# A two-block network on one core: compressed-key scores of two key heads in one step, and the last expert weights in fewer transfers

## The reference

```python
s = jnp.einsum('bgrcd,bgnd->bgrcn', qc, kc) * ATTN_SCALE        # kc: 31 compressed keys per key head
p_cmp = masked_softmax(s, cmp_end[None, :] <= tpos[:, None])     # max, exp, 0/1 mask, / max(sum, 1e-20)
o_cmp = jnp.einsum('bgrcn,bgnd->bgrcd', p_cmp, vc)
out = gc[..., 0:1] * o_cmp + ...
```

```python
a = jax.nn.silu(xb @ w_gate[e]) * (xb @ w_up[e])
return a @ w_down[e]
```

## Time and profile before

| | before |
|---|---|
| median of 3 runs | 2480.15 us (2478.76 to 2482.7) |
| the profiled execution | 2475.58 us, of which its span 2473.8 us |
| PE busy | 2260.6 us (91%) |
| DVE, ACT, POOL busy | 613.6, 331.4, 208.9 us |
| mean granted TensorE clock | 0.967 |
| moved by DMA | 552.44 MB |

### The profile page before, as it was taken

One profiled execution on the slowest core, in us unless ns is written; L12 is line 12 of the kernel. 1 busy time (PEld: TensorE's weight loads), 2 busy tenths in 40 slices (PEclk: granted clock), 3 DMA queues, 4 the chain that ended last, 5 costly groups with the idle time before them and its releaser, 6 DMA issues.

```text
span 2473.8 us, 20406 instructions
## 1 busy us (share of the span) xinstructions
PE 2260.6 (91%) x8284; PEld 1048.6 (42%) x8284; DVE 613.6 (25%) x1315; ACT 331.4 (13%) x668; POOL 208.9 (8%) x187
## 2 busy tenths in 40 slices
PE   8999999999999999999999999988788888878786
PEld 5554444445455544457644454333333333333332
DVE  2146544301623130032631142111111111111114
ACT  2014424202111100021010030000000000000001
POOL 0001111010333200000000000000000000000001
PEclk9999999999999999998999999999999988898998
DMA  6201010322232221128432429999999999999995
GB/s 270 85 35 68 35 68 8 146 102 85 85 106 88 112 105 68 68 73 134 151 123 85 170 108 407 425 426 427 426 426 426 427 426 426 424 426 423 423 397 219
DMA packets 70288, 552.44 MB, mean 223 GB/s; under 512 B 21416, under 2 KB 25640, under 8 KB 38768
## 3 DMA queue, kind: packets, MB, share of 16 engines
q1 hardware_dynamic: 43680, 515.49, 51.3%
q10 hardware_dynamic: 16432, 23.23, 3.1%
q0 software_dynamic: 10080, 12.38, 1.4%
HBM read 543.91 MB, written 35.68 MB: 234 GB/s over the span
## 4 chain that ended last, share of the span: by engine, by line
PE 70%; DMA 24%; DVE 2%; SPq 1%; ACT 1%; issue 1%; DVEq 0%; POOL 0%; ACTq 0%; POOLq 0%
PE ps L381 25%; DMA sb<-in_eu 11%; PE ps L457 9%; PE ps L1005 8%; PE ps L697 8%; DMA sb<-in_eg 6%; DMA sb<-in_ed 6%; PE ps L1034 4%; PE ps L400 2%; PE ps L855 2%; PE ps L629 2%; PE ps L542 1%; PE ps L575 1%; PE ps L569 1%; PE ps L676 1%
## 5 line engine op out<-in xcount | busy, mean ns | idle before, releaser
L381 PE MATMUL ps<-sb 128*128 128x512 f32 (+2 forms) x1536 | 613.8, 559 | 2.9 <-issue 1.4
L1005 PE MATMUL ps<-sb 128*64 128x512 f32 x2048 | 478.6, 623 | 89.4 <-DMA sb<-in_eu 63.3
L381 PEld LDWEIGHTS ps<-sb 128*128 128x128 f32 x1536 | 279.7, 190 | 317.4 <-issue 314.2
L1005 PEld LDWEIGHTS ps<-sb 128*64 128x64 f32 x2048 | 175.0, 143 | 372.3 <-issue 372.2
L1034 PE MATMUL ps<-sb 128*64 128x512 f32 x992 | 249.5, 661 | 38.0 <-DMA sb<-in_ed 26.2
L457 PE MATMUL ps<-sb 128*128 128x512 f32 x512 | 238.2, 604 | 0.0
L697 PE MATMUL ps<-sb 128*128 128x512 f32 x448 | 192.5, 592 | 0.7 <-issue 0.7
L1034 PEld LDWEIGHTS ps<-sb 128*64 128x64 f32 x992 | 81.0, 151 | 185.0 <-issue 166.8
L1448 DVE TENSOR_TENSOR sb<-sb 128x32 f32<-128x32 f32 (+10 forms) x292 | 115.4, 412 | 136.6 <-PE ps L663 83.2
L457 PEld LDWEIGHTS ps<-sb 128*128 128x128 f32 x512 | 92.1, 191 | 101.0 <-issue 99.7
L697 PEld LDWEIGHTS ps<-sb 128*128 128x128 f32 x448 | 85.0, 190 | 107.7 <-issue 107.7
(11 more groups left out here) (286 smaller groups left out, 1554.3 us busy)
## 6 DMA issues: line engine op xcount, KB each, us to landing
sb<-in_eg SPq DMA_DIRECT2D x64, 2048.0 KB, 33.0
sb<-in_eu SPq DMA_DIRECT2D x62, 2048.0 KB, 33.7
sb<-in_ed SPq DMA_DIRECT2D x62, 2048.0 KB, 33.9
sb<-in_m SPq DMA_DIRECT2D x16, 2048.0 KB, 7.3
sb<-in_mg SPq DMA_DIRECT2D x8, 1536.0 KB, 6.9
sb<-in_winF SPq DMA_DIRECT2D x5, 2048.0 KB, 7.3
sb<-in_mgg SPq DMA_DIRECT2D x4, 2048.0 KB, 7.3
sb<-in_wo SPq DMA_DIRECT2D x4, 2048.0 KB, 7.3
```

Source lines behind the costliest of these rows:

```text
L381: ins = pe.matmul(out, lhsT, rhs, start=k == 0, stop=k == len(pieces) - 1)
L1005: ins = pe.matmul(o[64 * e:64 * e + 64, :], x[:, k, 64 * e:64 * e + 64], weight(2 * mat + e)[:, 512 * k:512 * k + 512], start=k == 0, stop ...
```

## The change

Compressed scores: a step is now one block of 128 tokens with both key heads. PE issues the eight products with the heads in turn (j = 0: h = 0, h = 1, then j = 1 and so on), then three steps of the recurrence, then the eight transposes, then one step. DVE masks the two heads into one tile of eight rows of 31, and does every later pass on both at once (248 columns instead of 124 twice). ACT does one exponential for both. A block has its own tile `CT[i]`, so the wait for the transposes four passes earlier is gone.

Last pair: the up and the down matrix of the first expert come whole (2 MB). The up matrix of the second comes in two parts of 1 MB, its down matrix in parts of 1 MB, 512 KB and 512 KB. SP waits for each expert's slot just ahead of that expert's transfers.

```diff
 # PE, cmp_scores
+                    o = [open_tile(pe, ("cs", i, h), 2 + h) for h in range(2)]
+                    for j in range(4):
+                        for h in range(2):
+                            ins = pe.matmul(o[h][:, 31 * j:31 * j + 31], qT[64 * h:64 * h + 64, j, 128 * i:128 * i + 128],
+                                            kcT[64 * h:64 * h + 64, :], start=True, stop=True)
+                    yield 3
-                        yield 2
                         o = open_tile(pe, ("ct", i, h), 4 + h)
-                        pe.wait_ge(S("cprob"), 2 * i + h + 1)
+                        pe.wait_ge(S("cprob"), i + 1)
+                    yield 1
 # DVE, cmp_scores
-                        s3, st = view(CT[n % 4], 0, 4, 31), CT[n % 4][:, 124:128]
-                        if n > 3:
-                            dve.wait_ge(*T.full("ct", (n - 4) // 2, h))
+                    s3, st = view(CT[i], 0, 8, 31), CT[i][:, 248:256]
+                    after(own(dve.tensor_reduce(st, s3, op=ALU.max, axis=AX.X)))
+                    dve.tensor_tensor(s3, s3, bc(st, 2, 31), ALU.subtract).then_inc(S("csub"), 1)
+                    yield 2
+                    dve.wait_ge(S("cexp"), i + 1)
+                    after(tt(s3, s3, bc(ck("c01")[:, 31 * i:31 * i + 31], 1, 8), ALU.mult))
 # PE, last pair, up (k of 8) and down (k of 4)
-                    if parts and k % 2 == 0:
-                        pe.wait_ge(S(f"up{k // 2}"), 32)
+                    if parts and k == 0:
+                        pe.wait_ge(S("up0"), 16)
+                    if parts and k % 4 == 0:
+                        pe.wait_ge(S(f"up{1 + k // 4}"), 16)
-                    pe.wait_ge(S(f"last{k}"), 32)
+                    if k != 1:
+                        pe.wait_ge(S(f"last{max(k, 1)}"), 16)
+                    if k == 0:
+                        pe.wait_ge(S("last0"), 16)
 # SP, last pair
-            for e in range(2):
-                sp.wait_ge(*T.full(*W.ended[W.before[("ex", 6 * PAIRS - 4 + e)]]))
-            for k in range(4):
-                for e in range(2):
-                    sp.dma_start(slot("ex", 6 * PAIRS - 4 + e)[:, 1024 * k:1024 * k + 1024], ...
+            for mat, sem, parts in ((1, "up", (2048, 2048)), (2, "last", (2048, 1024, 1024))):
+                n = 6 * PAIRS - 6 + 2 * mat
+                sp.wait_ge(*T.full(*W.ended[W.before[("ex", n)]]))
+                sp.dma_start(slot("ex", n), EW[mat][2 * PAIRS - 2]).then_inc(S(f"{sem}0"), 16)
+                sp.wait_ge(*T.full(*W.ended[W.before[("ex", n + 1)]]))
+                for k, size in enumerate(parts):
+                    sp.dma_start(slot("ex", n + 1)[:, at_:at_ + size], ...
```

More of the change, by code:

```diff
@@ L1174, in cmp_scores @@
                 for i in range(4):
-                    for h in range(2):
-                        n = 2 * i + h
-                        s3 = view(CT[n % 4], 0, 4, 31)
-                        act.wait_ge(S("csub"), n + 1)
-                        act.activation(s3, s3, ACT.Exp, scale=0.125).then_inc(S("cexp"), 1)
-                        yield 2
-                        if h == 0:
-                            copy(("ct", i, 0), PCT[0:31, :, 128 * i:128 * i + 128],
-                                 T.ap("ct", i, 0)[0:31, :].rearrange("p (a b) -> p a b", a=4))
+                    s3 = view(CT[i], 0, 8, 31)
+                    yield 1
+                    act.wait_ge(S("csub"), i + 1)
+                    act.activation(s3, s3, ACT.Exp, scale=0.125).then_inc(S("cexp"), 1)
+                    yield 2
+                    copy(("ct", i, 0), PCT[0:31, :, 128 * i:128 * i + 128],
+                         T.ap("ct", i, 0)[0:31, :].rearrange("p (a b) -> p a b", a=4))
+                    yield 1
             def attention():
@@ L1623, in cmp_scores @@
                                           bc(ck("cneg")[:, 31 * i:31 * i + 31], 1, 4), ALU.add).then_inc(T.s("cs", i, h), 1)
+                    for h in range(2):
                         dve.wait_ge(*T.free("cs", i, h))
-                        after(own(dve.tensor_reduce(st, s3, op=ALU.max, axis=AX.X)))
-                        dve.tensor_tensor(s3, s3, bc(st, 2, 31), ALU.subtract).then_inc(S("csub"), 1)
-                        dve.wait_ge(S("cexp"), n + 1)
-                        after(tt(s3, s3, bc(ck("c01")[:, 31 * i:31 * i + 31], 1, 4), ALU.mult))
@@ L1629, in cmp_scores @@
-                        after(own(dve.tensor_reduce(st, s3, op=ALU.add, axis=AX.X)))
-                        after(ts(st, st, 1e-20, None, ALU.max))
-                        after(own(dve.reciprocal(st, st)))
-                        if n == 0:
-                            dve.wait_ge(S("gate"), 1)
-                        gcol = gate[:, i, :].rearrange("p (hd c) -> p hd c", c=3)[:, 4 * h:4 * h + 4, 0]
-                        after(tt(st, st, gcol, ALU.mult))
-                        dve.tensor_tensor(s3, s3, bc(st, 2, 31), ALU.mult).then_inc(S("cprob"), 1)
@@ new lines, in cmp_scores @@
+                    after(tt(s3, s3, bc(ck("c01")[:, 31 * i:31 * i + 31], 1, 8), ALU.mult))
+                    after(own(dve.tensor_reduce(st, s3, op=ALU.add, axis=AX.X)))
+                    after(ts(st, st, 1e-20, None, ALU.max))
+                    after(own(dve.reciprocal(st, st)))
+                    if i == 0:
+                        dve.wait_ge(S("gate"), 1)
+                    after(tt(st, st, gate[:, i, :].rearrange("p (hd c) -> p hd c", c=3)[:, :, 0], ALU.mult))
+                    dve.tensor_tensor(s3, s3, bc(st, 2, 31), ALU.mult).then_inc(S("cprob"), 1)
@@ L1642, in attention @@
+                    yield 1
+                    copy(("ct", i, 1), PCT[32:63, :, 128 * i:128 * i + 128],
+                         T.ap("ct", i, 1)[0:31, :].rearrange("p (a b) -> p a b", a=4))
+                    yield 1
             def attention():
@@ L2458, in sync_program @@
                     load(("ex", n), EW[k // 2][2 * q + k % 2])
[L2459 to L2470 removed]
+            for mat, sem, parts in ((1, "up", (2048, 2048)), (2, "last", (2048, 1024, 1024))):
[3 more added lines that the diff above has]
+                sp.wait_ge(*T.full(*W.ended[W.before[("ex", n + 1)]]))
+                at_ = 0
+                for k, size in enumerate(parts):
+                    sp.dma_start(slot("ex", n + 1)[:, at_:at_ + size], EW[mat][2 * PAIRS - 1][:, at_:at_ + size]).then_inc(S(f"{sem}{k + 1}"), 16)
+                    at_ += size
             sp.wait_ge(*T.full("g", PAIRS - 1))
```

29 lines of the change are left out of this document (7 added, 22 removed).

## The result

| | before | after |
|---|---|---|
| median | 2479.45 us (2473.11 to 2487.92, 6 runs) | 2461.15 us (2459.74 to 2463.95, 6 runs) |
| ratio, 95% interval | | 0.9927 [0.9907, 0.9947] |
| profiled execution, its span | 2475.58, 2473.8 us | 2463.95, 2462.0 us |

Before has three more runs here than it had when the forecast was made. The two profiled executions differ by 11.6 us, the medians by 18.3. The runs of one kernel spread over several microseconds, and the profiled execution of before was a short one, that of after a long one.

What follows compares the result with a forecast made beforehand. PE sets the pace up to slice 24, then waits for weights. Scores 5.5 us (waits 3.1, products 0.8, clock 1.6) plus last pair 3.0 make 8.5: from 2480.15 to 2471.6 us, range 2464.5 to 2478.

Steps and rivals of the forecast that it cites:

- the term for the products: Compressed scores: 64 product records with the heads in turn save 0.8 us, between none and 1.3.
- the distance between the profiled execution and the median: Whole kernel: the runs' median was taken to stay 4.6 us above the profiled execution, giving 2471.6 us.
- The clock: PE at the compressed scores: low clock costs 1.7 us instead of 3.3, so 1.6 saved.
- The waits: PE's gaps at the compressed scores: 0.5 us in the third block, 2.0 in the fourth, instead of 5.6; 3.1 saved.
- The last pair: Down products at the end: reordered, longer-row weight transfers gain 3.0 us, between a loss of 0.4 and a gain of 4.7.
- three quarters: Last pair: long-row weights take three quarters of the DMA service beside the gathers, so the first down product starts at 2440.3.
- 2 and 5: Last pair: SP has 2 and 5 issues to push instead of 8 and 8; nothing was counted for it.
- The limit that was set: Last pair: DVE's fourth gathered addition may come up to 3 us later, so a gain up to about 3 is safe.
- idle DMA time back in full: Rival, last pair: nothing waits in the down products, gain 9.1 us there, 14.6 in all, 2465.5 us; chance 0.15.
- Bytes shared as before: Rival, last pair: the end gives -0.4 to 0 us, 5.3 in all, 2474.9 us; chance 0.20.
- Scores little: Rival, compressed scores: DVE later, clock low as long as now; 1.9 us, nothing from the end, 2478.2 us; chance 0.12.
- the slower case: Rival, last pair: large transfers land late, end 6.5 us later, 2484.8 us with scores at their low end; chance 0.05.

Runs made afterwards that it cites:

- e13: Changed kernel with the score products in groups of two matmuls (four records) of one head in turn; 2460.09 us, one run.
- e2: New transfers of the last pair only, compressed scores as in the kernel before; 2472.25 us, 0.9993 of before.
- e8: Changed kernel with every score product done twice, four products of one head, then four of the other, and again; 2474.56 us, one run.
- e10: Changed kernel with the gating pass behind the scaling and two steps of PE's other work between products and transposes instead of three; 2472.88 us, 0.9972 of before.
- e1: New compressed scores only, transfers and waits of the last pair as in the kernel before; 2463.28 us, 0.9954 of before.
- e11: Changed kernel with the products ordered first of each head, then three of head 0, then three of head 1; 2460.97 us, one run.
- e3: Changed kernel with a block's eight products as four of one head, then four of the other; 2464.0 us, 0.9952 of before.
- e9: Changed kernel with DVE's gating pass moved behind the softmax scaling in each block; 2460.7 us, 0.9916 of before.
- e5: Changed kernel with every large transfer of the last pair cut to 4 KB rows, four 512 KB issues per 2 MB; 2466.91 us, 0.9957 of before.
- e12: Changed kernel with each of the last pair's two down matrices fetched whole by one 2 MB issue; 2465.11 us, 0.993 of before.
- e4: The changed kernel run again unchanged; 2463.68 us, 0.9959 of before.
- e6: Changed kernel with SP waiting for both experts' slots ahead of the first expert's transfer, as before the change; 2462.91 us, 0.9941 of before.
- e7: Changed kernel with every score product done twice, heads in turn, 32 records in a step; 2471.1 us, one run.

## Why the prediction was wrong

The direction and the place of each gain were right; the sum was too small, 8.5 us against 11.6 in the profiles. Two steps failed: the term for the products, and the distance between the profiled execution and the median, which was carried over as fixed. Step by step:

- **Products, the step that failed**: "may save up to 64 x 0.02 = 1.3 us, and at worst none; I take 0.8". Measured: eight groups of 1.00 became four of 1.01, 4.0 us. The rule of the Trainium skill ("TensorE: Matmul & The Clock Gate", Part 3), that matmuls in different row groups run at the same time, gave 4 and was dismissed; the trace agrees with it (1.01 us for 16 records, and 1.03 in e13). It was dismissed on a misread row. The four records at 191.11 are two pairs, with 0.19 to 0.21 us between the pairs; in nearly all later groups of that line, 542, the two records of a pair start 0.007 apart, so the trace of before held the overlap. I divided 0.42 by four records and got 0.105, near the 0.125 of the single head. But each of them moves 128 columns, the products 31. Pairs of 31 columns follow at 0.112. Two rows that differ in shape were compared as if only the order differed, and the bound "at best" was then taken from the same row. A true bound from rows would have been half of the 8.0 us, by the question whether anything in the trace excludes two records in one slot.
- **The clock**: "the clock falls once, for a shorter time", 1.6 saved. It did not fall there, 3.3 saved between these two profiles. But e2 shows the scores of before without the fall, so this part is not the change's in every execution, and e8 and e10 show falls with and without a wait ahead. In exchange the changed kernel's clock fell at 534.0 and 1083.5 and cost 1.7 each time, behind waits that before has too; e1 and e11 have no stretch at 534. So neither the 3.3 saved nor the 3.4 lost is shown to belong to the change.
- **The waits**: 2.5 us forecast (0.5 and 2.0), 2.8 measured (1.22 and 1.58), 2.8 saved for 3.1. The third block was 0.7 worse, and that too hangs on the products: they took 1.0 us where the forecast counted 1.8, PE was ready 0.8 earlier, and DVE's convolution, which the chain waits for, follows from PE's last projection. 0.5 + 0.8 = 1.3, measured 1.22; e3 shows the same the other way. The fourth was 0.4 better, and its cause was the one given, the gating pass in the chain (e9). That the cover decides was right, and e10 shows how near to the edge the change stands.
- **Transposes**: not in the sum. Two groups of four took 0.53 each up to what follows, one of eight takes 0.87: 0.8 us over the four blocks. With 4.0, 3.3 and 2.8 this makes 10.9, the measured 10.8.
- **The last pair**: "I take three quarters: 2440.3" for the first down product, 40.5 us after the earlier trace rows's up product, and a gain of 3.0. Measured 39.6 and 4.0; over twelve executions with the new end L is 46.96 to 49.35 (e5 and e12 left out), against 52.23 and 52.11 with the old one, and like compared with like 2.8 to 3.2, which is the forecast. One wait ahead of the first down product and none behind came as described (3.32 us for "some 4", 1.10 and 1.17 in e3 and e4). But no run shows the "three quarters" of the service that the number rests on, so a part of this hit may be luck: e5 shows that size matters and not by which way, and e6 that the earlier issue of the first matrix is worth nothing. The new code has 3 and 4 issues, not the "2 and 5" that the forecast names; no term used them. The limit that was set, DVE's fourth gathered addition, is reached in e3 and e4.
- **The rivals**: the first, idle DMA time back in full, needed no wait ahead of the down products; there is one. Bytes shared as before is excluded by L. Scores little and the slower case are excluded by d and by SP's short issues.
- **A misread row without weight**: the slices were read as 407 to 427 GB/s from the 25th on; the last two are 397 and 219. No term rests on it.
- **The median, the second step that failed**: "the median of the runs, 4.6 above it, to 2480.15 - 8.5 = 2471.6". Measured, the median stood 3.9 us above the profiled execution before (2479.45, six runs) and 2.8 below it after. The 11.6 us of the profiles, taken off 2480.15, give 2468.5, inside the range; the other 6.7 us of the medians' 18.3 are this offset. Two sets of runs of the same pair of kernels gave, by their ratios, 18.1 us [13.1, 23.1] and 10.1 [7.2, 12.9]. Executions also differ ahead of the change: some profiles (e3, e6, e7, e8, e12) come to the first product at 152 us instead of 143 to 145, behind a long stretch of low clock. The window of e12 there:

```profile
105.00:125.00 20.00, 18.61 (x76) 0.66 0.65 263
```

Both kernels' own profiles have 1.00 in it. So the gain lies between 7 and 23 us by the runs, and only the 11.8 between the two profiled spans have a place in the program.

## What to carry to other kernels

Where a matmul contracts 64 rows, put one of the other half of the rows beside it, or after four records (two matmuls here) at most: two heads then cost what one does. Before a price is read from a neighbouring row, check that it has the same number of moving columns, and look at the starts of single records, not at a group's mean. Count the cover, that is PE's other work, over a softmax chain that goes through two engines, and put nothing that waits for a third result into the middle of the chain.

## What the runs showed of the hardware

- Records of 64x31 products follow at 0.112 us in one half of the rows, and a second stream in the other half costs nothing (1.01 us for 16, 1.90 for 32). With 128 columns the pairs follow at 0.21, with 256 at 0.32. Three records of the second stream started ahead of the last record of the first, behind which they stand in the code, in e3, e11 and e13 alike (groups of 1.48, 1.25 and 1.03 us).
- The granted clock fell to the lower level (1.2 GHz) behind a wait of 2.29 us in one execution and not in another of the same code there (e2). Behind two other waits it fell in the changed kernel (2.26 and 3.52 us) and not in before (2.25 and 3.51), and once (e8) it fell with no wait ahead.
- Four issues of 512 KB, the fifth to eighth in a row, blocked SP for 16.46 us (e5), where issues of 1 MB at the same place took 0.33 to 0.43 each; the first three of 512 KB took 0.43 each as well.
